# A hybrid decoder layer with 32 experts: sample rows split over 128 partitions, light sides first, late loads, and another order of the last additions

## What is computed

```python
shift1, scale1, gate1, shift2, scale2, gate2 = split(silu(c) @ w_ada + b_ada)
q, k, v, B, C, h = split((x * (1 + scale1) + shift1) @ w_in)
mix = concat(rms(attention(q, k, v)), rms(B * conv3(C * h))) @ w_o
x = LN1(alpha * x + (1 + gate1) * mix)
u2 = x * (1 + scale2) + shift2
x = LN2(alpha * x + (1 + gate2) * MoE(u2))   # top-4 of 32 experts, clamped SwiGLU
```

## Time and profile before

| what | value |
|---|---|
| median of 3 runs | 1460.03 us (1457.73 to 1460.32) |
| profiled execution, its own time | 1456.86 us |
| its span | 1455.1 us |
| TensorE busy | 1387.9 us (95%) |
| VectorE busy | 496.2 us (34%) |
| ScalarE busy | 241.3 us (17%) |
| DMA | 523.72 MB, mean 360 GB/s |
| mean granted clock of TensorE | 0.978 of full speed |

### The profile page before, as it was taken

How to read it: one execution, slowest core, us unless ns; L and a number is a source line. 1 busy time by engine, 2 the same in 40 slices (tenths; PEclk the granted TensorE clock), 3 DMA queues, 4 the chain that set the end, 5 groups by cost and what they waited for, 6 DMA issues and landing times.

```text
span 1455.1 us, 21685 instructions
## 1 busy us (share of the span) xinstructions
PE 1387.9 (95%) x7813; PEld 571.8 (39%) x7814; DVE 496.2 (34%) x1091; ACT 241.3 (17%) x430; POOL 13.7 (1%) x22
## 2 busy tenths in 40 slices
PE   5899999999979999999999999999999999999993
PEld 2555666665443333333333333333333333333331
DVE  2210356554772222232233222223222322223336
ACT  0001334432021021111111101111111111111110
POOL 0000000000010000000000000000000000000000
PEclk9899999999979999999999999999999999999996
DMA  9949548999938699999999989999999999998941
GB/s 340 388 151 351 201 167 324 412 418 377 339 133 348 254 425 414 424 427 424 426 427 427 423 335 405 414 427 427 424 425 427 426 426 425 427 407 346 411 189 37
DMA packets 60900, 523.72 MB, mean 360 GB/s; under 512 B 8124, under 2 KB 8437, under 8 KB 20682
## 3 DMA queue, kind: packets, MB, share of 16 engines
q1 hardware_dynamic: 57696, 517.61, 86.8%
q0 software_dynamic: 1344, 4.90, 0.9%
q10 hardware_dynamic: 1834, 0.84, 0.3%
HBM read 519.87 MB, written 3.46 MB: 360 GB/s over the span
## 4 chain that ended last, share of the span: by engine, by line
PE 83%; DMA 10%; DVE 4%; issue 1%; SPq 1%; ACT 0%; DVEq 0%; ACTq 0%
PE ps L1714 29%; PE ps L1793 14%; PE ps L1315 6%; PE ps L1252 5%; PE ps L1619 5%; PE ps L1651 5%; DMA arena<-in_cache_v 4%; DMA arena<-in_w_up 4%; PE ps L1543 3%; DMA arena<-in_w_in 2%; PE ps L1706 2%; PE ps L1485 2%; PE ps L1312 2%; PE ps L1724 1%; PE ps L1642 1%
## 5 line engine op out<-in xcount | busy, mean ns | idle before, releaser
L1714 PE MATMUL ps<-arena 128*64 128x512 f32 x2048 | 449.8, 596 | 1.2 <-DMA arena<-in_w_up 1.1
L1714 PEld LDWEIGHTS ps<-arena 128*64 128x64 f32 x2048 | 144.2, 137 | 305.5 <-issue 301.6
L1793 PE MATMUL ps<-arena 128*64 128x512 f32 x1024 | 226.8, 595 | 2.5 <-issue 2.1
L1252 PE MATMUL ps<-arena 128*128 128x128 f32 (+4 forms) x1075 | 150.2, 280 | 19.6 <-DVE arena L734 10.8
L1186 DVE TENSOR_SCALAR arena<-ps 128x512 f32<-128x512 f32 (+1 forms) x35 | 24.2, 692 | 413.2 <-PE ps L1714 352.0
L1252 PEld LDWEIGHTS ps<-arena 128*128 128x128 f32 (+4 forms) x1075 | 115.2, 142 | 82.6 <-issue 45.6
L1793 PEld LDWEIGHTS ps<-arena 128*64 128x64 f32 x1024 | 71.0, 137 | 152.6 <-issue 152.6
L1619 PE MATMUL ps<-arena 128*64 128x512 f32 (+1 forms) x396 | 97.2, 609 | 1.1 <-DVE arena L1121 1.1
L679 ACT ACTIVATE arena<-arena 128x512 f32<-128x512 f32 (+1 forms) x35 | 22.1, 631 | 446.2 <-DVE arena L1186 446.2
L1134 DVE TENSOR_TENSOR arena<-arena,ps 128x512 f32<-128x512 f32 x33 | 22.8, 690 | 194.8 <-PE ps L1642 194.6
L1315 PE MATMUL ps<-arena 128*128 128x320 f32 x288 | 84.1, 444 | 4.3 <-DMA arena<-in_w_in 4.3
(11 more groups left out here) (240 smaller groups left out, 903.9 us busy)
## 6 DMA issues: line engine op xcount, KB each, us to landing
arena<-in_w_up SPq DMA_DIRECT2D x128, 2048.0 KB, 15.6
arena<-in_w_down SPq DMA_DIRECT2D x128, 1024.0 KB, 12.8
arena<-in_w_ada SPq DMA_DIRECT2D x12, 2048.0 KB, 17.8
arena<-in_cache_k SPq DMA_DIRECT2D x16, 1536.0 KB, 14.3
arena<-in_cache_v SPq DMA_DIRECT2D x16, 1536.0 KB, 9.7
arena<-in_w_in SPq DMA_DIRECT2D x6, 2048.0 KB, 20.5
arena<-in_cache_k SPq DMA_DIRECT2D x32, 192.0 KB, 12.8
arena<-in_cache_v SPq DMA_DIRECT2D x32, 192.0 KB, 10.8
```

The lines of the kernel that those rows point to most:

```text
L1252: return nc.tensor.transpose(o, i, ident[0:n, 0:n])
L1714: ins = mm(bank(part)[64 * h:64 * h + 64], xe_t[:, 0, at:at + 64], up_w[:, k, FF * part + 512 * h:FF * part + 512 * h + 512], start=False, ...
L1793: ins = mm(bank(3)[64 * h:64 * h + 64], a_t[:, 0, at:at + 64], dn_w[:, kk, 512 * h:512 * h + 512], start=kk == 0, stop=kk == KC - 1)
```

## The change

1. **Sample rows split.** Tile 2 of `u2`, `x1`, `mix`, `mod_s`, LN gains and biases holds its 64 rows on 128 partitions, 512 wide: partitions 64p to 64p+63 have, of each column half h, the quarter of 256 columns from 512h + 256p. `residual`, `finish` and the router's turns of tile 2 work on that. `bn_stats` gets one half on each side, and two small copies cross them. `gather` takes the sample rows with `sel_s`, zero outside its 64 rows, on all 128 rows of the array.
2. **Light sides first.** All `pe.If(x > 0)` of the items become `pe.If(x < 1)`, with the one-block side first.
3. **Late loads.** ScalarE waits for `ring_in[4]`, the first `w_in` block, before it issues the router weight and bias, now counted by `rw_in`. `mod_s` comes with 16 DMAs, the sample `x` with two, the LN2 rows with six.
4. **End.** TensorE adds `acc` (through the identity) and the weighted `b_down` into the banks ahead of each last scatter. ScalarE copies the gate rows of the prompt and of the sample group to SBUF. VectorE's `last_rows` goes, and `finish` reads the finished banks.

```diff
             act.dma_start(anti, t["anti"]).then_inc(tabc_in, 16)
-            act.dma_start(rw_sb, t["router_w"][0].rearrange("(k p) e -> p k e", p=128)).then_inc(tabc_in, 16)
-            act.dma_start(rb_sb[0:1, :], t["router_b"]).then_inc(tabc_in, 16)
+            act.wait_ge(ring_in[4], 16)
+            act.dma_start(rw_sb, t["router_w"][0].rearrange("(k p) e -> p k e", p=128)).then_inc(rw_in, 16)
+            act.dma_start(rb_sb[0:1, :], t["router_b"]).then_inc(rw_in, 16)
...
             for b in range(NB):
-                src = vectors[1 + b:2 + b, 0:3 * D].to_broadcast([NS, 3 * D]).rearrange("p (a b) -> p a b", a=3)
-                sp.dma_start(mod_s[NS * b:NS * b + NS], src).then_inc(mod_late, 16)
+                src = vectors[1 + b:2 + b, 0:3 * D].to_broadcast([NS, 3 * D])
+                for p in range(2):
+                    at = 64 * p + NS * b
+                    sp.dma_start(mod_s[at:at + NS].rearrange("q m (h j) -> q m h j", h=2),
+                                 src.rearrange("q (m h c) -> q m h c", m=3, h=2)[:, :, :, 256 * p:256 * p + 256]
+                                 ).then_inc(mod_late, 16)
...
-            for tt, (a, n) in enumerate(TILES):
+            act.wait_ge(g2_done, 1)
+            nc.scalar.copy(gate_rows[0], ps[:, 0:1024]).then_inc(g2_kept, 1)
+            act.wait_ge(g2_done, 2)
+            nc.scalar.copy(in_halves(gate_rows[1]), ps[:, 0:1024].rearrange("p (h n) -> p h n", h=2)[:, :, 0:256]
+                           ).then_inc(g2_kept, 1)
+            for tt in range(3):
                 act.wait_ge(var_ready, 6 + tt)
-                nc.scalar.activation(st[0:n, 36:37], st[0:n, 35:36], ACT.Sqrt).then_inc(sd_ready, 1)
+                nc.scalar.activation(st[:, 36:37], st[:, 35:36], ACT.Sqrt).then_inc(sd_ready, 1)
...
             modulate(0)
-            dve.wait_ge(mod_late, 128)
-            fold_norm(mod_s, 64)
+            V(v_.memset(sel_s, 0.0))
+            dve.wait_ge(mod_late, 256)
+            fold_norm_sample(0)
+            fold_norm_sample(1)
             keep_output(NB - 1)
...
+            def choose_rows(i):
+                for tt in range(2):
+                    v_.tensor_scalar(sel[:, tt, :], place[:, 0:CAP], rank_t[:, tt, bass.ds(i, 1)], None, ALU.is_equal)
+                for p in range(2):
+                    a, z = 64 * p, 64 * p + 64
+                    ins = v_.tensor_scalar(sel_s[a:z, p, :], place[a:z, 0:CAP], rank_t[a:z, 2, bass.ds(i, 1)], None,
+                                           ALU.is_equal)
+                ins.then_inc(sel_ready, 1)
...
-            def last_rows(tt):
+            def finish(tt):
+                w, gb = width(tt), ln2 if tt < 2 else ln2_s
+                dve.wait_ge(g2_kept, 1 if tt < 2 else 2)
                 dve.wait_ge(sc_done, items * 3 + tt + 1)
-                add_back(tt, ((6, 7), (4, 5), (2, 3))[tt]).then_inc(sc_added, 1)
...
-            last_rows(0)
-            last_rows(1)
-            dve.wait_ge(ln2_in, 32)
+            dve.wait_ge(ln2_in, 96)
             finish(0)
-            last_rows(2)
             finish(1)
             finish(2)
...
-                for tt, (_, n) in enumerate(TILES):
+                for tt in range(2):
                     for h in range(2):
-                        ins = mm(bank(4)[64 * h:64 * h + 64], sel[0:n, tt, 0:MAIN],
-                                 u2[0:n, tt, 512 * h:512 * h + 512], start=tt == 0, stop=tt == 2)
+                        mm(bank(4)[64 * h:64 * h + 64], sel[:, tt, 0:MAIN], u2[:, tt, 512 * h:512 * h + 512],
+                           start=tt == 0, stop=False)
+                for p in range(2):
+                    for h in range(2):
+                        ins = mm(bank(4, 256 * p, 256 * p + 256)[64 * h:64 * h + 64], sel_s[:, p, 0:MAIN],
+                                 u2[:, 2, 256 * h:256 * h + 256], start=False, stop=p == 1)
...
-                with pe.If(now_b > 0):
+                with pe.If(now_b < 1):
+                    up(1)
+                with pe.Else():
                     up(2)
-                with pe.Else():
-                    up(1)
...
+            def earlier_rows(tt, banks):
+                a = 128 * tt
+                for h in range(2):
+                    mm(bank(banks[h]), ident, acc[:, tt, 512 * h:512 * h + 512], start=True, stop=False)
+                for h in range(2):
+                    mm(bank(banks[h]), gt_sb[0:NE, a:a + 128], bd_sb[0:NE, 512 * h:512 * h + 512], start=False, stop=False)
+
+            def earlier_rows_sample(banks):
+                for h in range(2):
+                    for part in range(2):
+                        o, at = bank(banks[h], 0, 256)[64 * part:64 * part + 64], 512 * h + 256 * part
+                        mm(o, ident[:, 64 * part:64 * part + 64], acc[:, 2, 256 * h:256 * h + 256], start=True, stop=False)
+                        mm(o, gt_sb[0:NE, SEQ:NTOK], bd_sb[0:NE, at:at + 256], start=False, stop=False)
+
+            def last_rows(blocks):
+                scatter(0, (6, 7), blocks, first=False).then_inc(sc_done, 1)
+                earlier_rows(1, (4, 5))
+                scatter(1, (4, 5), blocks, first=False).then_inc(sc_done, 1)
+                earlier_rows_sample((2, 3))
+                scatter_sample((2, 3), blocks, first=False).then_inc(sc_done, 1)
...
             pe.wait_ge(sc_added, items * 3 + 1)
+            earlier_rows(0, (6, 7))
             pe.wait_ge(selt_ready, items + 1)
             pe.wait_ge(y_ready, items + 1)
             with pe.If(last_b > 0):
-                last_scatter(2)
+                last_rows(2)
             with pe.Else():
-                last_scatter(1)
-            for tt in (1, 2):
-                pe.wait_ge(sc_added, items * 3 + 1 + tt)
-                gate2(tt, (0, 6, 4)[tt])
+                last_rows(1)
+            pe.wait_ge(g2_kept, 1)
+            gate2(2, 0)
```

More of the change, by code:

```diff
@@ L177, in layer_kernel @@
         mod_p = view(W + 18 * D, 3, D)
-        mod_s = view(W + 21 * D, 3, D)
+        mod_s = view(W + 21 * D, 3, 512)
         p_bias = view(R2, HEADS, 256)
@@ L513, in _ @@
                 pool.dma_start(ln2[a], t[name][0:1, :].to_broadcast([128, D])).then_inc(ln2_in, 16)
+                for p in range(2):
+                    pool.dma_start(in_halves(ln2_s[a][64 * p:64 * p + 64]),
+                                   part_of(t[name][0:1, :].to_broadcast([64, D]), p)).then_inc(ln2_in, 16)
         @block.scalar
@@ new lines, in fold_norm, with fold_norm_sample @@
+            def fold_norm(mod, part, gain, bias):
+                V(v_.scalar_tensor_tensor(part, mod(2), 1.0, bias, ALU.add, ALU.mult))
+                V(v_.tensor_tensor(mod(1), mod(1), part, ALU.add))
+                V(v_.scalar_tensor_tensor(mod(2), mod(2), 1.0, gain, ALU.add, ALU.mult))
+            def fold_norm_sample(p):
+                a, z = 64 * p, 64 * p + 64
+                fold_norm(lambda m: in_halves(mod_s[a:z, m, :]), in_halves(mix[a:z, 1, 0:512]),
+                          part_of(ln1[0][a:z], p), part_of(ln1[1][a:z], p))
@@ L1139, in add_back @@
                 return ins
-            choose(0, "sel").then_inc(sel_ready, 1)
+            choose_rows(0)
             V(v_.tensor_copy(cnt[0:1, :], bank(1)[0:1, 0:NE]))
@@ L1493, in output_sample @@
                     lhs = o_t[:, c, a:a + n] if c < AC else y_c[:, c - AC, a:a + n]
-                    for h in range(2):
-                        ins = mm(bank(4)[64 * h:64 * h + 64], lhs, wo_sb[:, c, 512 * h:512 * h + 512],
+                    for p in range(2):
+                        ins = mm(bank(4)[64 * p:64 * p + 64], lhs, part_of(wo_sb[:, c, :], p),
                                  start=c == 0, stop=c == KC - 1)
@@ L1635, in turn_gathered, with scatter_sample @@
                 ins.then_inc(gathered_turned_done, 1)
-            def scatter_sample(banks, blocks, more=False):
+            def scatter_sample(banks, blocks, first=True):
                 for v in range(blocks):
@@ L1643, in scatter_sample, with scatter @@
                                      y_sb[64 * h:64 * h + 64, v, 256 * part:256 * part + 256],
-                                     start=v == 0, stop=v == blocks - 1 and not more)
+                                     start=first and v == 0, stop=v == blocks - 1)
                 return ins
-            def scatter(tt, banks, blocks, more=False):
+            def scatter(tt, banks, blocks, first=True):
                 for v in range(blocks):
@@ L1651, in scatter @@
                         ins = mm(bank(banks[h]), sel_t[64 * h:64 * h + 64, v, 128 * tt:128 * tt + 128],
-                                 y_sb[64 * h:64 * h + 64, v, :], start=v == 0, stop=v == blocks - 1 and not more)
+                                 y_sb[64 * h:64 * h + 64, v, :], start=first and v == 0, stop=v == blocks - 1)
                 return ins
-            def last_scatter(blocks):
-                for tt, banks in enumerate(((6, 7), (4, 5))):
-                    a, n = TILES[tt]
```

(18 more changed lines are left out.)

251 lines of the change are left out of this document (133 added, 118 removed).

## The result

The changed kernel takes 1450.23 us (median of five runs, 1449.68 to 1450.95) beside 1460.03 for the kernel before (five runs, 1457.73 to 1463.66): a ratio of 0.9937, 95% interval 0.9924 to 0.9950. The profiled execution has a span of 1448.1 us (1455.1 before) and a mean granted clock of 0.982 (0.978): 7.0 us between the two profiles.

| stretch | before | after | change | forecast |
|---|---|---|---|---|
| start to the sample tile's output product | 392.73 | 388.36 | -4.4 | -2.5 |
| from there to the first item (router, ranks) | 36.66 | 37.08 | +0.4 | -1.9 |
| item 0 | 39.67 | 34.01 | -5.7 | -1.4 (fetch) |
| items 1 to 30 | 922.00 | 921.78 | -0.2 | -1.1 |
| `gate2(0)` to the end | 35.1 | 38.1 | +3.0 | +2.1 |

What follows compares the result with a forecast made beforehand. TensorE was taken to bound most of the kernel, with DMA full in light items and VectorE strings in the middle and end. Terms -2.5 - 1.9 - 1.4 - 1.1 + 2.1 = -4.8 gave 1455.2 us from the median, range 1451 to 1460.5.

Steps and rivals of the forecast that it cites:

- Front: Kernel start: first w_in block lands up to 3.0 us sooner with loads held back; gain 2.5, bounds 1.4 to 3.3.
- Middle: Residual, router and kept rows: narrower VectorE instructions on 128 partitions start the first item sooner; gain 1.9, bounds 1.0 to 2.6.
- Fetch: First item: light side first removes one instruction-fetch stall and half covers the other; gain 1.4, bounds 3.6 gained, 1.5 lost.
- Loop: Item loop: gather 0.12 us shorter per light item, mostly hidden by full DMA queues; gain 1.1, bounds 0.2 and 2.4.
- End: After the last item: tile 0's root waits behind gate2(2), VectorE idles 8 us; loss 2.1, bounds 1.2 gained, 4.5 lost.
- The same change from the median: Whole kernel: the -4.8 reckoned on the profiled execution (1456.86) was applied to the median 1460.03, giving 1455.2.
- the 0.01 of the jumps: Item loop: each item pays for its jumps, 46 us over 31 later items, giving 1410; chance 0.01 of a rival's 0.08.
- faster: Whole kernel: measured time below 1457.1, given a chance of 0.63.
- ScalarE's order costs nothing: Kernel end: tile 0's root comes in time after all, end gains 5.8, total -12.7, 1447.3; chance 0.05.
- Modulation rows late: Before the output product: mod_s in 768 pieces of 1 KB lands late, delaying fold_norm(2); 1464 at 9 us late; chance 0.08.
- Swallowed gains: Early stretches and loop: clock rises where it did, cache loads set their own pace; total -0.8, 1459.2; chance 0.22.
- TensorE sets the items: Item loop: TensorE, not the loads, is the bound, so the whole 4 us of gather is kept; -7.7, 1452.3; chance 0.08.

Runs made afterwards that it cites:

- e2: Kernel before, with only router_w and router_b loads waiting behind ring_in[4], b_ada early; single execution, last w_ada product starts at 34.43 (31.98 before).
- e3: Kernel before, with only the four late b_ada loads waiting behind ring_in[4], router loads early; single execution, all but 0.7 us of e1's gain.
- e10: Changed kernel with e5's edit, and GpSimd's clearing of y_sb waiting for the sample tile's variance; ratio 0.9867 to the kernel before.
- e12: Changed kernel with e5's edit, GpSimd's later memset and 45 unused TensorE products in its waits; ratio 0.9871 to the kernel before.
- e6: Kernel before, with only the light side first in the nine branches of TensorE's item loop; ratio 0.9942, item 0 takes 32.64 us.
- e7: Changed kernel with the two-block side first again in TensorE's item loop; ratio 0.9981 to the kernel before, item 0 takes 39.00 us.
- e13: Changed kernel with e5's edit, later memset and 36 unused TensorE products sized to the waits; ratio 0.9899 to the kernel before.
- e8: Kernel before, loading half the columns of the last two w_down pieces in items 1 to 31; start of item 1 to item 31 takes 923.73 us.
- e9: Changed kernel, loading half the columns of the last two w_down pieces in items 1 to 31; start of item 1 to item 31 takes 920.93 us.
- e17: e13's version with 17 instead of 8 unused products before the item loop; median 1439.0 us, ratio 0.9831 to the kernel before.
- e11: Changed kernel with e5's edit and 45 unused TensorE products in its waits, memset not moved; ratio 0.9873 to the kernel before.
- e16: Same kernel as e5, run again: changed kernel with ScalarE's roots first; median 1445.69 us, ratio 0.9903 to the kernel before.
- e5: Changed kernel with tile 0's root ahead of the wait and second gate-row copy in ScalarE's end list; median 1441.47 us, ratio 0.9878.
- e1: Kernel before, with router_w, router_b and the four late b_ada loads waiting behind ring_in[4]; ratio 0.9982, -2.6 us.

## Why the prediction was wrong

- **Front, -2.5: right on average.** Up to 3.0 us of landing were forecast; the `w_in` product comes 3.0 earlier and the output product 2.8 in the mean over the traces. This pair drew 4.3, with the low clock shorter by 10 us: luck. The reason was half right: the engines were full, but of the two loads that it names only `b_ada` weighed (e2, e3), and the other queue was slower beside it. And the clock in rows 4 rose at 46.7, not at the window's end of 47.1.
- **Middle, -1.9: the wrong step, and the sign with it.** "TensorE's router of tile 2 ... keeps step, just" fails already at tile 1: at half clock its product takes 3.59 for 1.97 and VectorE waits 1.49 (0.46 and 1.03). The time of that product was taken at the full clock, where the trace before happened to have it; five of the eight traces of the old code do not. The "two crossing copies of 6 columns" (0.33 together) measured 1.55, because GpSimd's memset ran until 399.67; e10, with the memset later, has the copy at 0.17. The Trainium skill (SBUF — State Buffer, Who interferes with whom) has the two engines share a pair of ports under an exclusive lock, which a copy on VectorE can need and the loser waits out; the trace agrees, 1.38 against 0.17 us. I had not weighed it. 2.2 won - 1.2 - 1.5 leaves a loss of 0.4 to 0.5 (37.24 in seven traces of the new code, 36.71 in eight of the old). With both removed the forecast's size appears: from residual(2) to the ranks 16.47 us before, 14.22 in e12.
- **Fetch, -1.4: the failed step, the term that was mis-sized most, 5.7.** It alone is 4.3 us of the miss. I let one stand go and half of the other; both went, 3.6, and I had no term for the clock, which was low for 10.2 us around item 0's start before and for 6.8 after, though rows 4 showed it. The price set against it, jumps at the end of each light side, is nothing: 28.95 in e6 as before. The Trainium skill (Runtime: NRT & Kernel Launch, Instruction fetch mechanics) has a taken branch out of the small read-ahead window stall; here stands are seen on the first pass alone (in the kernel before, e7 and e13 for instance), and in e6 on no pass.
- **Loop, -1.1: right mechanism, its size a matter of dips.** -0.2 with one dip of 1.7 that the profile before had not; without it -1.9, and -2.5 in the mean over all traces, at and just beyond the far bound of 2.4. The cap by the loads is shown by e8 and e9, one execution each.
- **End, +2.1: right, +3.0.** The order, the place of the root and the stand came as written; the sample rows took 4.6 for 4.0, `finish(2)` 5.0 for 4.8.
- **"The same change from the median": the second failure.** The profiles differ by 7.0, the medians by 9.8. The kernel before was profiled in an execution without a single low stretch between unit 0 and the last item outside router and item 0; most of the other traces have one to five, most of which cost 1.7 us, and its other runs have mean clocks of 0.968 to 0.979. The changed kernel's profile had its two. A term of some 3 us for that draw was missing, and so was its width in the range.
- **The sum.** On the profiles -4.8 was forecast and -7.0 came: the fetch gave 4.3 too much and the front 1.9, the middle took 2.3 back and loop and end 1.8 together. That it came as near as that is partly luck, since the errors cancel. In the chances the 0.01 of the jumps is part of the rival's 0.08 and was counted twice: "faster" sums to 0.62.
- **Rivals.** ScalarE's order costs nothing: no, 8.57. Modulation rows late: no. Swallowed gains: in the middle and in the loop, yes; at the front, in single executions only. TensorE sets the items: in no stretch after the loads fill up.

That the low clock in router and item 0 goes when TensorE's waits are filled is shown by e13 and e17, and in part by e11 and e12. What decides the scattered short dips, and why e16 was in the router's low clock for 20 us where e5 had 17, stays open.

## What to carry to other kernels

Price each stretch at both clock levels before believing that a narrower string on one engine is a gain: the engine that "just keeps step" at full clock sets the pace at half. Where TensorE must wait for a known short time, unused products sized to that wait can be worth more than the work that was shortened; but in e13 a stand ahead of the gather took the gain back, and e11 and e12, with more products, gained nothing, so each such version wants a trace of its own. Read several traces of one kernel before pricing a clock stretch: one of them can lie 3 us off the median. And when the end of a kernel hangs on a short chain through several engines, read each engine's list in order: one copy ahead of a root cost 8.6 us here.

## What the runs showed of the hardware that I had not expected

- VectorE's small copy stood until GpSimd's memset was through (1.38 us, ending with it; 0.17 once the memset was later), while its arithmetic rows beside the memset ahead of that one (395.58 to 398.24) kept theirs, 0.69, 0.69 and 0.70.
- While the broadcast loads of `b_ada` (pieces of 2 KB) came in, their queue went at 258 GB/s of its own time and the queue beside it, also in pieces of 2 KB, at 291 instead of 368; 128 B pieces beside pieces of 8 KB left those at 410.
- With 36 (e13) or 45 (e17) short unused products in the waits the clock stayed at its upper level (2.4 GHz, 1.00 in the rows) where it otherwise ran at the lower (1.2 GHz) for 24 to 27 us.
- From the start of a fetch of one block of instructions to the first product behind it took 3.8 to 4.0 us in four versions. TensorE stood 3.47 us of it in e13 and 0.95 in e17, by nine products' difference ahead of the loop.
- Executions of one kernel differ by up to 9 us with their mean clock (e1: 1450.12 at 0.982, 1459.16 at 0.974).
